# A decoder layer in one kernel: the page keys as three fp32r products of high and low parts

## The chip, the cores and the metric

The kernel runs on one core of one Trainium2 chip. The metric is the device time of a run in microseconds (us).

## What is computed

One layer of a hybrid decoder, for a prompt of 512 tokens and for 8 sequences with one new token each. Two parts of it meet in the stage that is changed. The first is the attention of the new tokens over 8 x 2048 cached positions, which lie in pages of 128 positions with a latent of 512 and a rotated key of 64 numbers:

```python
def mla_keys(ckv, kpe, w_uk, g_k):
    k_nope = jnp.einsum('...c,chd->...hd', ckv, w_uk)
    k_pe = jnp.broadcast_to(kpe[..., None, :], k_nope.shape[:-1] + (D_ROPE,))
    return rms_norm(jnp.concatenate([k_nope, k_pe], axis=-1), g_k)
...
        ckv_all = jnp.concatenate([cache_ckv[pages].reshape(past, D_LATENT), ckv_i], axis=0)
        k = mla_keys(ckv_all, kpe_all, w_uk, g_k)
        sc = jnp.einsum('qhd,khd->hqk', qi, k).astype(jnp.float32) * scale
        p = jax.nn.softmax(sc, axis=-1).astype(ckv_all.dtype)
        o_lat = jnp.einsum('hqk,kc->qhc', p, ckv_all)
```

The second is the mixer of experts for the prompt, 8 heads of 16 experts a token, so 128 slots for each of 4 tiles of 128 tokens:

```python
        act = jax.nn.gelu(jnp.einsum('thkd,td->thk', u_tab[ids], hb), approximate=False)
        return jnp.einsum('thk,thkd->td', g * act, v_tab[ids])
```

## The kernel before

The function `experts` holds the last stage. Each engine has its own program there, written out by hand as a loop over slots x (0 to 511 for the prompt, 16 more for the samples), and semaphores join them. In a slot GpSimd (POOL) gathers 128 rows of `peer_u` (into `u`, a ring of 4) and 128 rows of `peer_v` (into `v`, a ring of 8), 512 KB each. VectorE (DVE) forms the dot product with the token's row (line 2608), and 6 slots later adds the `v` row times its coefficient (line 2508). ScalarE (ACT) turns four dot products into coefficients with a gelu (line 2341), VectorE weights them (line 2621), and from slot 62 on every eighth `v` row is added by TensorE (PE, line 2140). VectorE also searches the experts of the units to come, 16 parts a unit, one part a slot.

The pages of the cache run in the same loop. Page g starts in slot `page_slot[g]` = 62 + 376 g / 128, so every 2.94 slots, 128 pages in slots 62 to 435, 16 pages a sequence. SyncE (SP) loads a page into a ring of 24 (lines 1986 to 1988), a reload waits until the sequence that held the place is weighed. In the slot of page g TensorE turns page g+1 (`turn`, 4 transposes at line 2109, one of the rotated keys at line 2110), and ScalarE copies the result into `ckvT` (line 2320) and `kpeT` (line 2321). `page_bank` forms the key products of page g in this slot and the next two, one PSUM bank a slot: 4 chunks of the latent times 392, 384 and 256 columns (384, 384 and 264 in every other sequence) of `wx`, which holds w_uk and on one side the queries folded through it; the product with the rotated queries stands at line 2127. ScalarE squares the heads of a bank one slot later (`page_squares`, line 2332, with its sum read in a second instruction) and copies the scores out (line 2334). At a sequence's end VectorE, ScalarE and TensorE make the softmax and the weighted sum (lines 2531 to 2555).

Engines follow their own order, so who waits holds up all that stands behind it. The gelu of a slot stands in ScalarE's program behind the squares of the slots before it, the squares wait for TensorE's bank (semaphore `keyed`), TensorE's bank waits until ScalarE has drained the same bank of the page before (`drained`), and VectorE waits for the coefficients (`gelued`).

A matmul of fp32 operands stands in the trace as two instructions. In the projections of the earlier stages the kernel already forms three fp32r products (`products`, lines 352 to 354) of operands that `lower` (line 346) has split into a rounded high part and the rest.

```python
    pe.matmul(out, w_hi, x_hi, start=first, stop=False)
    pe.matmul(out, w_hi, x_lo, start=False, stop=False)
    return pe.matmul(out, w_lo, x_hi, start=False, stop=last)
```

## Time and profile before

| | |
|---|---|
| runs | 2862.69, 2867.62, 2875.89 us |
| median | 2867.62 us |
| span of the profiled execution | 2876.5 us |
| own time of the profiled execution beside its span | not given apart; the span is used |
| mean granted TensorE clock | 0.917 |
| TensorE busy | 2433.7 us (85%) |
| VectorE busy | 2059.7 us (72%) |
| ScalarE busy | 916.1 us (32%) |
| GpSimd busy | 1410.3 us (49%) |
| stage `experts` | from about 1042 us to the end |
| pages | from about 1320 to 2580 us |

The span runs from the first to the last instruction of one profiled execution. Busy times are sums over all stages, which have different limits; a change in one stage has to be read in that stage. A matmul's end is modelled, so that TensorE's busy time is not its time at peak.

### The profile page before, as it was taken

What the parts mean: (1) busy time and instruction counts of PE and PEld (TensorE: products, weight loads), DVE (VectorE), ACT (ScalarE), POOL (GpSimd) and SP (SyncE); (2) the same over time, 40 slices, a digit from 0 to 9 for tenths busy, and PEclk for the clock granted to TensorE, in tenths of its full rate; (3) what the DMA queues carried; (4) which work ended last, traced back from release to release, by engine and by line L of the source; (5) the groups of instructions that cost most, each with busy time, mean ns of one, the idle gap of its engine ahead of it and who ended that gap; (6) DMA issues with size and microseconds to landing.
All of it is one profiled execution on the core that took longest, in us unless ns stands there. A gap on an engine that the chain in (4) does not pass through costs nothing.

```text
span 2876.5 us, 36363 instructions
## 1 busy us (share of the span) xinstructions
PE 2433.7 (85%) x11529; PEld 1646.0 (57%) x11529; DVE 2059.7 (72%) x4017; ACT 916.1 (32%) x3611; POOL 1410.3 (49%) x1184
## 2 busy tenths in 40 slices
PE   5999997968989986887999999989989989983353
PEld 3999997854456643444656556655655556552120
DVE  4665887955531118897887888887887879887687
ACT  3431003234330002213444444534444435440110
POOL 1121331210000005776767677767876667776575
PEclk8999998989999998998999999999999999995576
DMA  6324765544025558999989999898989899989997
GB/s 197 91 80 144 216 205 150 136 124 120 11 89 177 177 188 293 401 388 385 348 291 375 348 352 376 307 366 290 400 306 370 293 376 364 347 319 358 401 347 300
DMA packets 375326, 777.12 MB, mean 270 GB/s; under 512 B 46577, under 2 KB 181538, under 8 KB 375097
## 3 DMA queue, kind: packets, MB, share of 16 engines
q0 software_dynamic: 155568, 566.17, 52.7%
q1 hardware_dynamic: 198442, 183.99, 20.2%
q10 hardware_dynamic: 21124, 24.63, 2.6%
q8 instruction: 92, 1.51, 0.2%
q14 instruction: 100, 0.82, 0.1%
HBM read 745.38 MB, written 29.50 MB: 269 GB/s over the span
## 4 chain that ended last, share of the span: by engine, by line
PE 27%; issue 9%; another core or an unknown queue 9%; DMA 6%; DVE 4%; SPq 3%; POOL 2%; ACT 1%; POOLq 0%; DVEq 0%; ACTq 0%
PE mix_pair L2125 19%; DMA mix_u<-in_peer_u,mix_ids 5%; PE mix_pair L2048 2%; DVE mix_acc L2508 2%; PE mix_pair L2140 2%; POOL mix_v L2038 1%; DVE mix_u L2608 1%; SPq L1988 1%; PE mix_pair L2109 1%; DMA pag_kpe<-in_cache_kpe 1%; SPq L1987 1%; PE mix_pair L2127 1%; POOL mix_u L2031 1%; PE mix_pair L2077 1%
## 5 line engine op out<-in xcount | busy, mean ns | idle before, releaser
L2125 PE MATMUL mix_pair<-pag_wx,pag_ckvT 128*128 128x384 f32 (+3 forms) x3072 | 980.7, 467 | 39.4 <-issue 31.3
L2125 PEld LDWEIGHTS mix_pair<-pag_wx,pag_ckvT 128*128 128x128 f32 x3072 | 571.6, 194 | 336.1 <-issue 66.2
L2038 POOL DMA_INDIRECT mix_v<-in_peer_v,mix_ids x512 | 643.5, 1257 | 234.2 <-issue 171.0
L2031 POOL DMA_INDIRECT mix_u<-in_peer_u,mix_ids x512 | 595.6, 1163 | 316.7 <-issue 141.0
L2608 DVE CUSTOM_DVE_ANT_0 mix_u<-mix_u,mix_h 128x1024 f32<-128x1024 f32 x512 | 622.5, 1216 | 172.0 <-DMA mix_u<-in_peer_u,mix_ids 155.1
L2508 DVE SCALAR_TENSOR_TENSOR mix_acc<-mix_v,mix_coef,mix_acc 128x1024 f32<-128x1024 f32 x452 | 577.9, 1278 | 0.0
L2332 ACT ACTIVATE mix_pair<-mix_pair 128x128 f32<-128x128 f32 x1024 | 269.6, 263 | 445.3 <-PE mix_pair L2125 259.1
L379 POOL CAST inp_w_hi<-inp_w 128x1024 fp32r<-128x1024 f32 x74 | 112.2, 1517 | 377.1 <-DMA inp_w<-in_w_in 286.3
L2332 ACT ACTIVATION_READ_ACCUMULATOR mix_pair<-mix_pair 128x1 f32 x1024 | 191.7, 187 | 0.0
L2014 POOL IOTA mix_count_i<- 128x16 int32 x1 | 0.1, 134 | 376.2 <-POOLq L88 376.2
L2140 PE MATMUL mix_pair<-mix_v,mix_diag 128*128 128x512 f32 x224 | 116.5, 646 | 62.8 <-ACT mix_diag L2349 35.1
L352 PE MATMUL stp_ps<-inp_h_hi,inp_w_hi 128*128 128x260 f32 x512 | 148.0, 289 | 13.6 <-DVE inp_w_lo L346 10.4
L354 PE MATMUL stp_ps<-inp_h_hi,inp_w_lo 128*128 128x260 f32 x512 | 146.4, 286 | 0.0
L353 PE MATMUL stp_ps<-inp_h_lo,inp_w_hi 128*128 128x260 f32 x512 | 146.1, 285 | 0.0
L1677 DVE TENSOR_TENSOR mrg_gate<-mrg_psB,mrg_gate 128x520 f32<-128x520 f32 x8 | 5.6, 699 | 184.8 <-PE mrg_psB L1638 184.8
L2320 ACT ACTIVATE pag_ckvT<-mix_pair 128x512 f32<-128x512 f32 x128 | 75.6, 591 | 169.3 <-DMA scn_ce<-keep_acs 68.5
L2341 ACT ACTIVATE mix_coef<-mix_dots 128x4 f32<-128x4 f32 x128 | 25.9, 202 | 306.5 <-DVE mix_dots L2608 279.9
L352 PE MATMUL cnv_ps<-inp_h_hi,inp_w_hi 128*128 128x260 f32 x416 | 120.8, 290 | 0.0
L354 PE MATMUL cnv_ps<-inp_h_hi,inp_w_lo 128*128 128x260 f32 x416 | 118.4, 285 | 0.0
L353 PE MATMUL cnv_ps<-inp_h_lo,inp_w_hi 128*128 128x260 f32 x416 | 118.3, 284 | 0.0
L2077 PE MATMUL mix_pair<-chs_h2T,chs_wq 128*128 128x512 f32 (+2 forms) x352 | 115.9, 488 | 0.9 <-ACT chs_h2T L2304 0.6
L1638 PE MATMUL mrg_psB<-frt_x,mrg_wb 128*128 128x260 f32 x512 | 114.3, 384 | 0.0
(520 smaller groups left out, 4092.1 us busy)
## 6 DMA issues: line engine op xcount, KB each, us to landing
inp_w<-in_w_in SPq DMA_DIRECT2D x74, 512.0 KB, 4.2
pag_ckv<-in_cache_ckv SPq DMA_DIRECT2D x88, 256.0 KB
mrg_w_ada<-in_w_ada SPq DMA_DIRECT2D x8, 2048.0 KB, 9.9
chs_wq<-in_peer_wq SPq DMA_DIRECT2D x11, 1024.0 KB, 16.5
all_shared<-in_cache_ckv SPq DMA_DIRECT2D x40, 256.0 KB
keep_proj<-stp_out ACTq DMA_DIRECT2D x32, 260.0 KB
ada_w_ada<-in_w_ada SPq DMA_DIRECT2D x4, 2048.0 KB, 12.8
stp_st<-in_state_ssm POOLq DMA_DIRECT2D x8, 1024.0 KB, 6.9
```

The source lines that it names most:

```text
L352: pe.matmul(out, w_hi, x_hi, start=first, stop=False)
L353: pe.matmul(out, w_hi, x_lo, start=False, stop=False)
L354: return pe.matmul(out, w_lo, x_hi, start=False, stop=last)
L1638: last = pe.matmul(psB[:, b, s, 0:HALF], wb[:, b, k, :], yT[:, k, s * HALF:(s + 1) * HALF], start=(k == 0), stop=(k == KI - 1))
L2031: pool.indirect_dma_start(u[:, x % UR, :], None, u_rows, bass.IndirectOffsetOnAxis(at, 0)).then_inc(u_in[x % UR], 16)
L2038: pool.indirect_dma_start(v[:, y % VR, :], None, v_rows, bass.IndirectOffsetOnAxis(at, 0)).then_inc(v_in[y % VR], 16)
L2077: last = pe.matmul(bank[2 + side][:, 0:w], wq[:, n % 2, k, side * P:(side + 1) * P], h2T[:, k, cols], start=(k == 0), stop=(k == KD - 1))
L2125: last = pe.matmul(to, ckvT[:, g % 2, k, :], wx[:, k, lo:hi], start=(k == 0), stop=(k == KL - 1))
L2140: last = pe.matmul(psV[:, c, :], diag[:, d % 2, :], v[:, r, c * 512:(c + 1) * 512], start=(x == first_on_pe[t]), stop=(x == last_on_pe[t]))
L2332: last = act.activation(psN[j][:, at:at + NOPE], psN[j][:, at:at + NOPE], ACT.Square, accum_out=ss[:, b % 2, t, h:h + 1])
L2508: dve.scalar_tensor_tensor(acc[:, :], v[:, r, :], c, acc[:, :], ALU.mult, ALU.add).then_inc(v_used[r], 1)
L2608: dve.tensor_tensor_reduce(u[:, r, :], u[:, r, :], h2[:, t % 2, :], 1.0, 0.0, ALU.mult, ALU.add, dots[:, t % 2, slot:slot + 1]).then_inc(u ...
```

## The change

The key products of a page are made of three fp32r products in place of one fp32 product. Both operands are split: `wx` into `wx_hi` (ScalarE rounds) and `wx_lo` (VectorE subtracts, line 346), in slots 24 to 41 for w_uk, and a slot after each copy of a sequence's queries. A page's high part `ckvT_hi` is the copy that ScalarE makes of the turned page, rounded on writing. One slot after the turn, TensorE multiplies it by minus the identity (`minus`) on top of the turned page in the same PSUM bank, which leaves the rest there, and ScalarE copies that as `ckvT_lo`. The next page's turn waits for that copy.

The second set of operands takes room. Four places of the ring of pages move into the scores of tile 0 (`sc_first`), and SP loads them only when that tile's 8 units are searched; `w_uk` is loaded into `shared`, and the first page waits until it is split; `ids` and `gate` keep two tiles, not four; `hot` shares the place of the two candidate tiles; w_uv is loaded behind all pages; the samples' small tiles lie where the pages were, so their zeroing and loads come after the last page, and `mul_s` is made at TAIL + 8, not TAIL + 2 (TAIL is slot 460). The scores of tile 0 and 1 are copied apart.

```diff
-            SHARED = 8
-            ckv, kpe = e.sb("ckv", [P, NPG - SHARED, LAT]), e.sb("kpe", [P, NPG, ROPE])
+            SHARED, SCORED = 8, 4
+            ckv, kpe = e.sb("ckv", [P, NPG - SHARED - SCORED, LAT]), e.sb("kpe", [P, NPG, ROPE])
             ckv_shared = shared[:, :].rearrange("p (r c) -> p r c", r=SHARED)
-            ckvT, kpeT = e.sb("ckvT", [P, 2, KL, P]), e.sb("kpeT", [ROPE, 2, P])
-            wx = e.sb("wx", [P, KL, WX])
+            ckv_scored = flat2(sc_first[:, :]).rearrange("p (r c) -> p r c", r=SCORED)
+            ckvT_hi, ckvT_lo = e.sb("ckvT_hi", [P, 2, KL, P], F32R), e.sb("ckvT_lo", [P, 2, KL, P], F32R)
+            kpeT, minus = e.sb("kpeT", [ROPE, 2, P]), e.sb("minus", [P, P], F32R)
+            e.sb("unused", [P, P])
+            wx_lo, wx_hi = e.sb("wx_lo", [P, KL, WX], F32R), e.sb("wx_hi", [P, KL, WX], F32R)
+            w_uk = shared[:, :].rearrange("p (k n) -> p k n", k=KL)
...
-        score_of = lambda unit: sc[:, unit]
-        page_rows = lambda r: ckv[:, r, :] if r < NPG - SHARED else ckv_shared[:, r - (NPG - SHARED), :]
+        score_of = lambda unit: sc_first[:, unit] if unit < PH else sc[:, unit - PH]
+        OWN = NPG - SHARED - SCORED
+        page_rows = lambda r: ckv[:, r, :] if r < OWN else ckv_shared[:, r - OWN, :] if r < OWN + SHARED else ckv_scored[:, r - OWN - SHARED, :]
...
-        score_rows = sc[:, :, :, :].rearrange("p (t h) s n -> p t h s n", t=TT)
+        score_rows = sc[:, :, :, :].rearrange("p (t h) s n -> p t h s n", t=TT - 1)
+        scores_to = lambda ts, h: sc_first[:, h:h + 1] if ts[0] == 0 else score_rows[:, ts[0] - 1:ts[0] - 1 + len(ts), h]
...
+        rest_at = {page_slot[0] - 1: 0, **{x + 1: g + 1 for g, x in enumerate(page_slot) if g + 1 < PAGES}}
+        queries_at = {page_slot[NT * (b - 1) + 1]: b for b in range(2, TS)}
+        WX_AT = (24, 29, 35, 40)
...
             sp.wait_ge(res_summed, 2 * TT)
-            sp.dma_start(wx[:, :, QW:QW + H * NOPE], heads("w_uk")).then_inc(wx_in, 16)
+            sp.dma_start(w_uk, heads("w_uk")).then_inc(wx_in, 16)
...
             sp.wait_ge(scored, len(steps))
+            sp.wait_ge(wx_lowered, KL)
             for g in range(PAGES):
+                if g == OWN + SHARED:
+                    sp.wait_ge(found, PARTS * PH)
                 if g >= NPG:
                     sp.wait_ge(weighed, (g - NPG) // NT + 1)
-                if g == PAGES - 24:
-                    sp.wait_ge(found, PARTS * 16)
-                    sp.dma_start(w_uv, heads("w_uv")).then_inc(uv_in, 16)
                 page = sp.value_load(table[0:1, g:g + 1], min_val=0, max_val=A["cache_ckv"].shape[1] - 1)
                 sp.dma_start(page_rows(g % NPG), A["cache_ckv"][0, bass.ds(page, 1)].rearrange("a p c -> (a p) c")).then_inc(page_in[g % NPG // 4], 16)
                 sp.dma_start(kpe[:, g % NPG, :], A["cache_kpe"][0, bass.ds(page, 1)].rearrange("a p c -> (a p) c")).then_inc(page_in[g % NPG // 4], 16)
             sp.wait_ge(found, PARTS * 24)
-            sp.dma_start(gate1_s, ada_s(2)).then_inc(gate1_in, 16)
-            sp.dma_start(mul_s, ada_s(4)).then_inc(scale_in, 16)
+            sp.dma_start(w_uv, heads("w_uv")).then_inc(uv_in, 16)
             sp.wait_ge(y_stored, 16 * (TT - 1))
             sp.dma_start(gain_s, A["g_ffn"].to_broadcast([TS, D])).then_inc(scale_in, 16)
             sp.wait_ge(weighed, TS)
+            sp.dma_start(mul_s, ada_s(4)).then_inc(scale_in, 16)
             sp.dma_start(w_a[:, :, :], wide("w_br_a")).then_inc(a_in, 16)
+            sp.dma_start(gate1_s, ada_s(2)).then_inc(gate1_in, 16)
+            sp.dma_start(x1s[:, :], A["x_sample"].rearrange("b t d -> (b t) d")).then_inc(x1s_in, 16)
             sp.dma_start(w_out_lo[:, :, :], wide("w_out")[:, 0:KD // 2, :]).then_inc(out_in, 16)
             sp.dma_start(w_out_hi, wide("w_out")[:, KD // 2:KD, :]).then_inc(out_in, 16)
             sp.wait_ge(muls_made, 1)
...
             def turn(g):
                 r = g % NPG
                 pe.wait_ge(page_in[r // 4], 128 * (g // NPG + 1))
-                after(pe, copied, 2 * g)
+                after(pe, copied, 3 * g)
                 for k in range(KL):
-                    pe.transpose(psT[:, k * P:(k + 1) * P], page_rows(r)[:, k * P:(k + 1) * P], K["ident"][:, :])
+                    pe.matmul(psT[:, k * P:(k + 1) * P], page_rows(r)[:, k * P:(k + 1) * P], K["ident"][:, :], start=(k == 0), stop=(k == KL - 1), is_transpose=True,
+                              skip_group_check=True)
                 pe.transpose(psK[0:ROPE, 0:P], kpe[:, r, :], K["ident"][:, :]).then_inc(turned, 1)
+
+            def page_rest(g):
+                pe.wait_ge(copied, 3 * g + 2)
+                pe.wait_ge(negated, 1)
+                pe.matmul(psT, minus[:, :], ckvT_hi[:, g % 2].rearrange("p k n -> p (k n)"), start=False, stop=True, skip_group_check=True).then_inc(rest_made, 1)
             def page_bank(g, j):
                 b, odd = g // NT, g // NT % 2
                 lo, hi = ((QW * odd, 392), (392, 776), (776, WX - QW * (1 - odd)))[j]
                 if j == 0:
                     if g % NT == 0:
-                        pe.wait_ge(q_set, b + 1)
+                        pe.wait_ge(q_low, b + 1)
                     if g == 0:
-                        pe.wait_ge(wx_in, 16)
+                        pe.wait_ge(wx_lowered, KL)
                         pe.wait_ge(s_copied, scores_before[-1])
-                    pe.wait_ge(copied, 2 * g + 2)
+                    pe.wait_ge(copied, 3 * g + 3)
                 after(pe, drained, 3 * (g - 1) + j + 1)
                 to = psN[j][:, QW * odd * (j == 0):QW * odd * (j == 0) + hi - lo]
                 for k in range(KL):
-                    last = pe.matmul(to, ckvT[:, g % 2, k, :], wx[:, k, lo:hi], start=(k == 0), stop=(k == KL - 1))
+                    last = products(pe, to, (ckvT_hi[:, g % 2, k, :], ckvT_lo[:, g % 2, k, :]), (wx_hi[:, k, lo:hi], wx_lo[:, k, lo:hi]), k == 0, k == KL - 1)
                     if k == 0 and j == 2 * odd:
                         pe.matmul(psN[0][:, 0:QW] if not odd else psN[2][:, 256:256 + QW], kpeT[:, g % 2, :], L["q_rope"][:, b, :],
                                   start=False, stop=False)
                     g = page_at[x]
                     if g + 1 < PAGES:
                         turn(g + 1)
+                if x in rest_at:
+                    page_rest(rest_at[x])
                 for g, j in bank_at.get(x, ()):
                     page_bank(g, j)
...
             def page_copy(g):
                 act.wait_ge(turned, g + 1)
                 after(act, keyed, 3 * (g - 1))
-                act.activation(ckvT[:, g % 2].rearrange("p k n -> p (k n)"), psT, ACT.Copy).then_inc(copied, 1)
+                act.activation(ckvT_hi[:, g % 2].rearrange("p k n -> p (k n)"), psT, ACT.Copy).then_inc(copied, 1)
                 act.activation(kpeT[:, g % 2, :], psK[0:ROPE, 0:P], ACT.Copy).then_inc(copied, 1)
+
+            def page_rest(g):
+                act.wait_ge(rest_made, g + 1)
+                act.activation(ckvT_lo[:, g % 2].rearrange("p k n -> p (k n)"), psT, ACT.Copy).then_inc(copied, 1)
...
+                if x in WX_AT:
+                    k = WX_AT.index(x)
+                    act.wait_ge(wx_in, 16)
+                    act.activation(wx_hi[:, k, QW:QW + H * NOPE], w_uk[:, k, :], ACT.Copy).then_inc(wx_rounded, 1)
...
                     page_squares(g, j)
+                if x in rest_at:
+                    page_rest(rest_at[x])
                 if x == page_slot[0] - 2:
+                    act.activation(minus[:, :], K["ident"][:, :], ACT.Copy, scale=-1.0).then_inc(negated, 1)
                     page_copy(0)
...
                         residual(t)
                     if x == NORM_AT[t]:
                         norm(t)
+                if x - 1 in WX_AT:
+                    k = WX_AT.index(x - 1)
+                    lower(dve, wx_hi[:, k, QW:QW + H * NOPE], wx_lo[:, k, QW:QW + H * NOPE], w_uk[:, k, :], wx_rounded, wx_lowered, k + 1)
+                if x == 31:
+                    for b in range(2):
+                        cols = slice(0, QW) if b == 0 else slice(WX - QW, WX)
+                        lower(dve, wx_hi[:, :, cols], wx_lo[:, :, cols], L["q_lat"][:, :, b, :], q_set, q_low, b + 1)
+                if x - 1 in queries_at:
+                    b = queries_at[x - 1]
+                    cols = slice(0, QW) if b % 2 == 0 else slice(WX - QW, WX)
+                    lower(dve, wx_hi[:, :, cols], wx_lo[:, :, cols], L["q_lat"][:, :, b, :], q_set, q_low, b + 1)
...
-                if x == TAIL + 2:
+                if x == TAIL:
+                    dve.tensor_copy(mineT[:, :, :], K["ident"][0:TS, 0:TS].unsqueeze(1).to_broadcast([TS, P // TS, TS]))
+                if x == TAIL + 8:
                     dve.wait_ge(scale_in, 32)
                     dve.scalar_tensor_tensor(mul_s, mul_s, 1.0, gain_s, ALU.add, ALU.mult).then_inc(muls_made, 1)
```

TensorE's program, two slots of a page in the first sequence (`all_ident` the identity, `pag_wx` the weights, `pag_ckvT` the turned page; the last number is the columns). Before:

```order
L2109 MATMUL mix_pair<-all_ident,pag_ckv 128x128 x4
L2110 MATMUL mix_pair<-all_ident,pag_kpe 64x128
L2125 MATMUL mix_pair<-pag_wx,pag_ckvT 128x392
L2127 MATMUL mix_pair<-all_q_rope,pag_kpeT 128x8
L2125 MATMUL mix_pair<-pag_wx,pag_ckvT 128x392 x3
L2125 MATMUL mix_pair<-pag_wx,pag_ckvT 128x384 x4
```

After, from the rope product of a page to the first product of its second bank:

```order
L2146 MATMUL mix_pair<-all_q_rope,pag_kpeT 128x8
L352 MATMUL mix_pair<-pag_wx_hi,pag_ckvT_hi 128x392
L353 MATMUL mix_pair<-pag_wx_lo,pag_ckvT_hi 128x392
L354 MATMUL mix_pair<-pag_wx_hi,pag_ckvT_lo 128x392
...
L2129 MATMUL mix_pair<-pag_ckvT_hi,pag_minus 128x512
L352 MATMUL mix_pair<-pag_wx_hi,pag_ckvT_hi 128x384
```

Each product has become three, and the product that makes the rest of the page turned last (line 2129) stands between the first bank and the second.

ScalarE's program around one page (`mix_coef<-mix_dots` is the gelu, `mix_ss` the squares' sums). Before:

```order
L2320 ACTIVATE pag_ckvT<-mix_pair 128x512
L2321 ACTIVATE pag_kpeT<-mix_pair 64x128
L2388 ACT_TABLE_LOAD
L2388 ACTIVATE mix_exps,mix_total<-mix_exps 128x16
L2341 ACT_TABLE_LOAD
L2341 ACTIVATE mix_coef<-mix_dots 128x4
L2328 ACTIVATE mix_kpe_sq,mix_kss<-pag_kpe 128x64
L2332 ACTIVATE mix_pair,mix_ss<-mix_pair 128x128 x8
```

After:

```order
L2341 ACTIVATE pag_ckvT_hi<-mix_pair 128x512
L2342 ACTIVATE pag_kpeT<-mix_pair 64x128
L2374 ACTIVATE mix_diag<-all_ident,mix_coef 128x128
L2353 ACTIVATE mix_pair,mix_kss<-pag_kpe 128x64
L2357 ACTIVATE mix_pair,mix_ss<-mix_pair 128x128 x3
L2346 ACTIVATE pag_ckvT_lo<-mix_pair 128x512
L2366 ACTIVATE mix_coef<-mix_dots 128x4
L2357 ACTIVATE mix_pair,mix_ss<-mix_pair 128x128 x3
```

The copy of the rest (line 2346) stands behind the squares of the first bank, and here ahead of a gelu.

## Rows read from the trace of the kernel before

**Rows 1.** The page of the profile, its first line.
```profile
span 2876.5 us, 36363 instructions
```

**Rows 2.** Windows: busy us (x instructions) by engine, clock, DMA.
```profile
core 0: us, PE busy (x) PEld busy (x) DVE busy (x) ACT busy (x) POOL busy (x), PEclk, DMA share, GB/s
1200.00:1320.00 120.00, 85.95 (x284) 48.99 (x283) 105.67 (x203) 21.28 (x48) 92.59 (x76) 0.87 1.02 387
1320.00:2580.00 1260.00, 1183.19 (x4470) 737.57 (x4470) 1038.19 (x2088) 571.41 (x2967) 902.72 (x743) 0.97 0.92 345
```

**Rows 3.** Windows of line 2608 alone, two records a slot.
```profile
1200.00:1320.00 120.00, 45.40 (x74) 0.87 1.02 387
1320.00:2580.00 1260.00, 455.98 (x746) 0.97 0.92 345
```

**Rows 4.** Waits of VectorE, 1320 to 2580 us: us, times, longest.
```profile
DVE mix_u L2608 <- DMA mix_u<-in_peer_u,mix_ids: 85.8, 89, 3.2
DVE mix_coef L2621 <- ACT mix_coef L2341: 56.2, 14, 8.0
DVE mix_rstd L2534 <- ACT mix_rstd L2379: 34.0, 5, 9.1
DVE mix_u L2608 <- issue: 13.2, 22, 2.1
DVE all_o_lat L2555 <- remote: 11.2, 3, 4.4
DVE mix_coef L2621 <- issue: 10.3, 4, 6.7
DVE mix_rstd L2531 <- ACT mix_raw L2334: 4.3, 2, 3.4
DVE mix_rstd L2531 <- issue: 3.7, 1, 3.7
DVE mix_part_sum L2548 <- ACT mix_s L2382: 3.1, 3, 1.6
```

**Rows 5.** Timeline around 2084 to 2104 us: start, us, instruction, idle before.
```profile
2083.53 4.47 PE L2125 MATMUL mix_pair<-pag_wx,pag_ckvT 128*128 128x384 f32 x16
2089.54 2.24 PE L2125 MATMUL mix_pair<-pag_wx,pag_ckvT 128*128 128x392 f32 x6
2087.26 0.26 ACT L2332 ACTIVATE mix_pair<-mix_pair 128x128 f32<-128x128 f32 x1 [2.65 <-PE mix_pair L2125]
2092.26 0.26 ACT L2332 ACTIVATE mix_pair<-mix_pair 128x128 f32<-128x128 f32 x1 [4.01 <-PE mix_pair L2125]
2099.41 0.26 ACT L2332 ACTIVATE mix_pair<-mix_pair 128x128 f32<-128x128 f32 x1 [5.92 <-remote]
2103.13 0.16 DVE L2621 TENSOR_TENSOR mix_coef<-mix_coef,mix_gate 128x4 f32<-128x4 f32 x1 [5.47 <-ACT mix_coef L2341]
```

**Rows 6.** Timeline of TensorE, one page from turn to turn.
```profile
1904.20 0.60 PE L2109 MATMUL mix_pair<-all_ident,pag_ckv 128*128 128x128 f32 x4
1904.75 5.77 PE L2125 MATMUL mix_pair<-pag_wx,pag_ckvT 128*128 128x384 f32 x18
1910.45 0.38 PE L2127 MATMUL mix_pair<-all_q_rope,pag_kpeT 64*128 64x8 f32 x2
1910.77 1.60 PE L2125 MATMUL mix_pair<-pag_wx,pag_ckvT 128*128 128x264 f32 x6
1912.20 0.60 PE L2109 MATMUL mix_pair<-all_ident,pag_ckv 128*128 128x128 f32 x4
```

**Rows 7.** Timeline of TensorE in the projection, three fp32r products a chunk.
```profile
401.45 0.28 PE L353 MATMUL stp_ps<-inp_h_lo,inp_w_hi 128*128 128x260 f32 x1
...
403.95 0.28 PE L353 MATMUL stp_ps<-inp_h_lo,inp_w_hi 128*128 128x260 f32 x1
```

**Rows 8.** Groups by line and form, whole span: busy us, mean ns.
```profile
L2125 PEld LDWEIGHTS mix_pair<-pag_wx,pag_ckvT 128*128 128x128 f32 x3072 | 571.6, 194 | 336.1 <-issue 66.2 <-ACT mix_pair L2332 11.0 <-ACT mix_raw L2334 6.0
L346 DVE TENSOR_TENSOR inp_w_lo<-inp_w,inp_w_hi 128x1024 fp32r<-128x1024 f32 x74 | 96.8, 1319 | 16.1 <-POOL inp_w_hi L379 15.7
L2320 ACT ACTIVATE pag_ckvT<-mix_pair 128x512 f32<-128x512 f32 x128 | 75.6, 591 | 169.3 <-DMA scn_ce<-keep_acs 68.5 <-PE mix_pair L2110 63.3 <-PE mix_pair L2125 20.5
```

70 lines of the change are left out of this document (36 added, 34 removed).

## The prediction

> **What bounds the kernel now.** I first looked for the stretch in which the page products stand. The windows [rows 2] show it from 1320 to 2580 us: 1260 us, with TensorE busy 1183 us (94%), VectorE 1038 us (82%), the DMA queues at 0.92 of their time and 345 GB/s. Nothing is at its limit on its own. In the 120 us ahead of it, with no pages, TensorE is at 72%, VectorE at 88% and the queues at 1.02 and 387 GB/s. The instructions of the dot product alone [rows 3] give the pace: two records are one slot, so 37 slots in 120 us (3.24 us each) and 373 slots in 1260 us (3.38 us each). The first number is the higher for its bytes: weights for the queries are loaded there.
>
> VectorE carries each slot, so its idle time is what can be won. Its waits in the stretch [rows 4] fall in two parts. It waits for gathered rows 85.8 + 13.2 = 99 us. It waits for something that ScalarE has to deliver 56.2 + 34.0 + 11.2 + 10.3 + 4.3 + 3.7 + 3.1 = 122.8 us, in 14 + 5 + 3 + 4 + 2 + 1 + 3 = 32 waits, 3.8 us each. 1038 + 99 + 123 is the stretch of 1260 us (one more wait, of 2.5 us, is not among the rows). ScalarE itself is busy less than half of it (571 us in [rows 2]). It is late because the squares of a page stand ahead of the gelu in its order, and they wait for TensorE.
>
> [Rows 5] show one such case, and with it the doubtful point of this forecast. TensorE's 16 instructions from 2083.53 (the second and third bank of a page) have ended by 2088.00, and those of 2089.54 belong to the next page's first bank. ScalarE begins the squares of the first bank at 2087.26, of the second at 2092.26 and of the third (two heads, the last of the page) at 2099.41, waiting 2.65, 4.01 and 5.92 us, though by its records TensorE was done 4 us and 11 us before the last two. VectorE then stands 5.47 us for the coefficients. So a part of the 123 us is not TensorE working too long, but its word arriving late at ScalarE, and shorter products do not shorten that.
>
> **The change, part by part.** *Key products.* [Rows 6] hold one page from turn to turn: 1904.20 to 1912.20, 8.00 us. The transposes take 0.55 (to 1904.75), the rope product 0.32 (1910.45 to 1910.77), and 7.13 us are left for the 12 fp32 products over 4 x (384 + 384 + 264) = 4128 columns, 1.73 ns a column. Three fp32r products of the same kind as the new ones (high x high, low or high weights changing at each) run in the projection [rows 7]: from the record at 401.45 to that at 403.95, 21 products of 260 columns in 2.50 us, 0.119 us each, 0.458 ns a column. Three are 1.37 ns a column, 5.67 us a page. That frees 1.46 us. If the part of a product that does not grow with its columns is large, 384 columns cost less than this line says; 5.4 us is the other end.
>
> A rule of the Trainium skill speaks against the change: TensorE: Matmul & The Clock Gate, "Measured speedup vs the span model", says that a weight load overlaps a running product only when the row groups differ. By it, and the same page's 128 / 1.2 = 107 ns a load (my estimate from the page's figures), the page's 36 loads would lie bare: 3.9 us, and a page would take longer than before. The trace disagrees: the 0.119 us of [rows 7] hold product and load.
>
> *The low part.* One product of 512 columns at 0.458 ns is 0.23 us. Net: 1.46 - 0.23 = 1.2 us a page, 128 pages: 156 us less work for TensorE, 1027 us in place of 1183. It would be busy about 85% of a stretch of 1210 us. At 72% the granted clock was 0.87, here it is 0.97 [rows 2]: even 0.93 would give back only 4% of 1027 us, which the slack covers.
>
> *ScalarE.* One more copy of 128x512 a page, 591 ns [rows 8]: 128 x 0.59 = 76 us more, 647 us of 1260. It stands behind the first bank's squares, ahead of the next gelu. On its own it is covered.
>
> *One more handover.* Before, TensorE turned page g+1, and needed ScalarE's copy three slots later. Now, one slot later, it must make the rest from that copy before it may start the second bank of page g, and ScalarE must wait for the rest before it goes on to the gelu. The handovers from TensorE to ScalarE go from 4 to 5 a page, and this one has a slot of cover, not three. Queued behind it on TensorE are two banks, behind ScalarE's wait the squares and the gelu, for which VectorE waits. Its price does not stand in the trace: the near bound is nothing (0.6 us of copy behind 1.9 us of products), the far one 4.01 us [rows 5]. I take it in the sum as eating part of the relief, below.
>
> *VectorE.* Four low parts of w_uk, 128x1024, 1319 ns each [rows 8]: 5.3 us, at slots 25 to 41, where it is idle 12% of the time; I charge 3 us. ScalarE's four rounding copies are hidden there. Eight small low parts of the queries: some 1 us in all. Five more score copies and the moved memsets, which were 3 small ones ahead of the stage: nothing, under VectorE's 12% idle and the gathers.
>
> *Queues.* SP loads 20 pages at first, not 24; pages 20 to 23 wait for the 8th search (slot 103), and are turned from slot 117 on. 14 slots x 3.38 = 47 us are in hand for 4 pages. If that cover went, the price would be a burst of 4 pages, 1.15 MB, at 345 GB/s: 3.3 us. w_uv comes behind the last page, at about slot 420 for slot 460. In the tail mul_s comes after the last weighing, and VectorE forms it at TAIL+8, two slots before anything needs it late. The bytes of the tail are the same. I put all this at nothing.
>
> **The sum.** How much of the 123 us comes back? Not less than nothing, not more than all of it. The case in [rows 5] says that the waits consist of TensorE's lateness plus late arrival. A page now is 1.2 us shorter, and between the slot at which TensorE falls behind and VectorE's wait lie one or two pages: 1.2 x 1.4 = 1.7 us less in each of 32 waits, 54 us. Less 4 us for VectorE's added work: 50 us. The profiled execution has a span of 2876.5 us [rows 1]; it would come to 2826.5. The runs shown have a median of 2867.62, 8.9 us under that span, so I forecast **2818 us**. A difference under 0.5% (14 us) can't be told from no change.
>
> **Rivals.**
> - *Everything comes back.* If TensorE's load is the whole cause, VectorE will be idle only as much as ahead of the pages: 105.67 of 120 us busy, and 1038 / 0.881 = 1179 us, a gain of 81 less 4, so 2790. With every one of the 123 us gone it is 2749. For it: TensorE at 94%. Against it: ScalarE's waits that begin after TensorE's records end. I give 0.22 to 2743 to 2793.
> - *Nothing measurable.* The late words decide alone, or the gathers take back what ScalarE gives: the 434 MB of the stretch (1260 us x 345 GB/s) at 387 GB/s need 1123 us, so the queues do not forbid a gain, and this is less likely. 2853 to 2882, chance 0.15.
> - *Slower: the added handover.* A page waits twice in series for TensorE's word (turned, then rest), and TensorE sends more instructions (36 products in place of 24 records a page). If one page in four takes an extra 4.01 us on VectorE's path, 32 x 4 = 128 us stand against 50, so 2868 + 78 = 2946. It decides from 64 us on, one page in eight. For it: 2.65, 4.01 and 5.92 us in one page. Against: the first bank's 1.9 us lie between copy and rest. Chance 0.25.
> - *Bare weight loads.* Twelve more loads a page at 194 ns each [rows 8] would cost 2.3 us, 1.1 more than the page wins, 140 us in all if TensorE then sets the pace: 3008. The rule named above is this one; [rows 7] leave it 0.02.
> - The forecast itself, 2793 to 2853, has 0.36.
>
> **The numbers.** Faster by over 0.5%: 0.36 + 0.22 = 0.58. Within: 0.15. Slower: 0.27. The range 2765 to 2895 leaves out about 0.07 below, where nearly all of the 123 us would have to come back, and about 0.12 above, where the handover fails at more than one page in seven.
>
> **What would show it.** In the profile after: the records of a page's products from turn to turn 6.8 us apart where TensorE is not held up (wrong if above 7.3); TensorE's share of the stretch near 85%; VectorE's waits for ScalarE near 70 us, in place of 123, and its waits for gathered rows at 99 or more. If TensorE now waits for the copy at the new product (an idle row of over 50 us there), or ScalarE for the rest, the slower rival is at work. If the stretch ends 80 us or more sooner, the lateness of TensorE's word was only its load. The forecast is wrong too if the clock falls below 0.9 in the stretch, or if the pages 20 to 23 are late.

## The result

The changed kernel takes 2905.54 us (median of 4 runs, 2897.26 to 2928.30), the kernel before 2869.88 on the same chip (4 runs, 2862.69 to 2875.89). The ratio is 1.0126 [1.0084, 1.0168]: 36 us slower, where 50 us faster was forecast. The forecast missed, on the sign too.

The page of the changed kernel, its first line, one of its three groups of key products, and the new product of 512 columns (L2129):

```profile
span 2896.7 us, 39969 instructions
...
L352 PE MATMUL mix_pair<-pag_wx_hi,pag_ckvT_hi 128*128 128x384 f32 (+3 forms) x1536 | 545.1, 355 | 5.6 <-issue 2.8
...
L2129 PE MATMUL mix_pair<-pag_ckvT_hi,pag_minus 128*128 128x512 f32 x128 | 64.9, 507 | 113.6 <-ACT pag_kpeT L2342 87.6
```

The profiled execution is 20.2 us longer than that before (2896.7 against [rows 1]); the other 16 us of the difference of medians are seen in no trace. TensorE's idle time stands at L2129, where it waits for ScalarE's copy of the page that it has turned.

The windows of the same two stretches as [rows 2]:

```profile
core 0: us, PE busy (x) PEld busy (x) DVE busy (x) ACT busy (x) POOL busy (x), PEclk, DMA share, GB/s
1200.00:1320.00 120.00, 91.55 (x308) 51.09 (x306) 115.09 (x222) 26.04 (x60) 92.45 (x78) 0.92 1.03 391
1320.00:2580.00 1260.00, 1089.21 (x6076) 956.43 (x6077) 1030.57 (x2084) 625.91 (x3055) 905.19 (x741) 0.92 0.93 344
```

In the stage TensorE fell from 94% to 1089 / 1260 = 86%, as forecast. VectorE did no more in the same 1260 us than before (1031 us, 1038 before). So 94 us less of TensorE's time bought VectorE nothing. Its waits tell what happened to the 122.8 us of [rows 4]:

```profile
engine line waited for: us in total, times, longest us
DVE mix_u L2653 <- DMA mix_u<-in_peer_u,mix_ids: 72.0, 73, 2.7
DVE mix_coef L2666 <- ACT mix_coef L2366: 58.2, 12, 8.1
DVE mix_u L2653 <- issue: 34.3, 47, 2.6
DVE pag_wx_lo L346 <- ACT pag_wx_hi L2408: 25.5, 4, 9.1
DVE pag_wx_lo L346 <- issue: 7.4, 2, 5.6
DVE mix_part_sum L2591 <- ACT mix_s L2414: 7.1, 3, 3.2
DVE mix_rstd L2574 <- ACT mix_pair L2357: 6.6, 2, 4.2
DVE all_o_lat L2598 <- remote: 5.5, 2, 2.8
```

What the forecast counted as ScalarE's is waited for 58.2 + 25.5 + 7.4 + 7.1 + 6.6 + 5.5 us in these rows. With the small ones that are left out (3.6 + 3.1 + 2.1 + 1.6 + 1.0) it is 122 us, as much as before. The old waits did shrink, to 89 us, and 33 us stand at a new place: L346, the low parts of the queries, where VectorE waits for ScalarE's high part. I had put that edit at some 1 us in all. Rows are waited for 106 us, 99 before. One of the groups, `all_o_lat`, isn't ScalarE's: VectorE waits there for a product of TensorE (semaphore `o_turned`), 11.2 us before and 5.5 + 3.6 = 9.1 us now.

TensorE's timeline of a page, one product to a row (start, duration, instruction, idle time before it):

```profile
start us, us, engine line op out<-in xcount [idle before <-releaser]
...
1603.00 0.60 PE L2122 MATMUL mix_pair<-all_ident,pag_ckv 128*128 128x128 f32 x4
...
1604.07 0.34 PE L352 MATMUL mix_pair<-pag_wx_hi,pag_ckvT_hi 128*128 128x384 f32 x1
...
1605.13 0.34 PE L352 MATMUL mix_pair<-pag_wx_hi,pag_ckvT_hi 128*128 128x384 f32 x1
...
1605.49 0.33 PE L354 MATMUL mix_pair<-pag_wx_hi,pag_ckvT_lo 128*128 128x384 f32 x1
1606.33 0.50 PE L2129 MATMUL mix_pair<-pag_ckvT_hi,pag_minus 128*128 128x512 f32 x1 [0.51 <-issue]
...
1610.75 0.49 PE L2122 MATMUL mix_pair<-all_ident,pag_ckv 128*128 128x128 f32 x3
```

From turn to turn (L2122) 7.75 us pass. Of these about 0.7 go to the wait ahead of L2129 (the next product could have begun at 1605.66), so the page alone takes some 7.1, under the 7.3 at which the step would have been wrong. Six products with their own weight loads stand between 1604.07 and 1605.13: 0.177 us each, 0.46 ns a column at a granted clock of 1.00, as taken from [rows 7]. By the rule of the Trainium skill that I weighed (TensorE: Matmul & The Clock Gate; it stands in "The mechanism", not in the section that the prediction names) the loads would lie bare; the trace disagrees here too. The same section of the Trainium skill also lets a load into the background weight buffer run ahead, a case that I left out; the trace shows the overlap, and not which buffer was loaded.

The same place in the program as [rows 5], first TensorE, then ScalarE, then VectorE:

```profile
2084.54 0.34 PE L354 MATMUL mix_pair<-pag_wx_hi,pag_ckvT_lo 128*128 128x392 f32 x1
2084.72 0.40 PE L2129 MATMUL mix_pair<-pag_ckvT_hi,pag_minus 128*128 128x512 f32 x1
...
2086.89 0.34 PE L354 MATMUL mix_pair<-pag_wx_hi,pag_ckvT_lo 128*128 128x384 f32 x1
...
2088.37 0.28 PE L354 MATMUL mix_pair<-pag_wx_hi,pag_ckvT_lo 128*128 128x256 f32 x1
2093.76 1.09 PE L2122 MATMUL mix_pair<-all_ident,pag_ckv 128*128 128x128 f32 x4 [5.11 <-ACT pag_ckvT_lo L2346]
```
```profile
2092.13 0.26 ACT L2357 ACTIVATE mix_pair<-mix_pair 128x128 f32<-128x128 f32 x1 [8.31 <-remote]
...
2093.02 0.59 ACT L2346 ACTIVATE pag_ckvT_lo<-mix_pair 128x512 fp32r<-128x512 f32 x1
2099.28 0.26 ACT L2357 ACTIVATE mix_pair<-mix_pair 128x128 f32<-128x128 f32 x1 [5.67 <-remote]
```
```profile
2103.37 0.16 DVE L2666 TENSOR_TENSOR mix_coef<-mix_coef,mix_gate 128x4 f32<-128x4 f32 x1 [7.13 <-ACT mix_coef L2366]
```

The first bank's last product ends at 2084.88. ScalarE, idle, begins that bank's squares at 2092.13, 7.25 us later. The second bank's products were over by 2087.23, and its squares begin at 2099.28, 5.67 us after ScalarE's last instruction. TensorE stands 5.11 us for the low copy (L2346), and VectorE 7.13 us for the coefficients (5.47 in [rows 5]). Nothing that TensorE computes is late here by these records; its word is. The trace also keeps the time of each semaphore's update: the one for the first bank stands at 2092.11, 7.23 us after the bank's last record and 0.02 us before the squares.

I counted these late words in the traces: a square of a bank, or the copy of a turned page, that begins over 0.6 us after both the last product's record and ScalarE's own last instruction have ended. The usual distance is 0.04 us. For a copy, the products of the page two before it must have ended too, for it waits for their word as well. The changed kernel has 72 late ones among 384 first squares of a bank (189 us) and 19 among 128 copies (49 us). The kernel before has 54 (136 us) and 25 (72 us). For 71 of the 72, an update of the bank's semaphore is recorded within 0.04 us before the squares begin: TensorE's word comes late, ScalarE doesn't start late.

VectorE gets late words from TensorE too. In the kernel before all 11.2 us of `all_o_lat` in [rows 4] are three such waits, in the changed one 5.5 us are two, the first of them (`remote` is explained at the last set of runs):

```profile
1868.28 0.19 DVE L2598 TENSOR_TENSOR all_o_lat<-mix_pair,mix_share 128x32 f32<-128x32 f32 x1 [2.68 <-remote]
```

### The profile page after: what moved, and what is told of

The parts are those of the page before. It is cut to its first block, busy times and chain, and to the rows that moved or that the text cites. A ratio compares the mean times of both kernels' runs of the same rounds, so it can differ in the third digit from the quotient of the medians.

```text
span 2896.7 us, 39969 instructions
## 1 busy us (share of the span) xinstructions
PE 2348.5 (81%) x13193; PEld 1875.7 (65%) x13193; DVE 2063.5 (71%) x4029; ACT 983.9 (34%) x3749; POOL 1413.3 (49%) x1184
## 4 chain that ended last, share of the span: by engine, by line
PE 17%; issue 13%; DVE 12%; DMA 10%; POOL 4%; another core or an unknown queue 3%; ACT 3%; SPq 1%; POOLq 0%; ACTq 0%; DVEq 0%
DMA mix_u<-in_peer_u,mix_ids 7%; DVE mix_acc L2540 5%; DVE mix_u L2653 5%; PE mix_pair L354 3%; PE mix_pair L352 3%; PE mix_pair L353 3%; POOL mix_u L2044 2%; POOL mix_v L2051 2%; PE mix_pair L2061 2%; DMA all_shared<-in_peer_keys 1%; ACT mix_pair L2357 1%; PE mix_pair L2159 1%; PE mix_pair L2090 1%; PE mix_pair L2122 1%
## 5 line engine op out<-in xcount | busy, mean ns | idle before, releaser
L2044 POOL DMA_INDIRECT mix_u<-in_peer_u,mix_ids x512 | 608.0, 1188 | 312.4 <-issue 145.1
L2051 POOL DMA_INDIRECT mix_v<-in_peer_v,mix_ids x512 | 632.1, 1235 | 250.9 <-issue 173.9
L352 PE MATMUL mix_pair<-pag_wx_hi,pag_ckvT_hi 128*128 128x384 f32 (+3 forms) x1536 | 545.1, 355 | 5.6 <-issue 2.8
L353 PE MATMUL mix_pair<-pag_wx_lo,pag_ckvT_hi 128*128 128x384 f32 (+3 forms) x1536 | 512.6, 334 | 3.4 <-issue 3.4
L354 PE MATMUL mix_pair<-pag_wx_hi,pag_ckvT_lo 128*128 128x384 f32 (+3 forms) x1536 | 512.4, 334 | 1.0 <-issue 1.0
L352 PEld LDWEIGHTS mix_pair<-pag_wx_hi,pag_ckvT_hi 128*128 128x128 f32 x1536 | 307.1, 200 | 13.7 <-issue 6.5
L353 PEld LDWEIGHTS mix_pair<-pag_wx_lo,pag_ckvT_hi 128*128 128x128 f32 x1536 | 307.2, 200 | 13.5 <-issue 7.1
L354 PEld LDWEIGHTS mix_pair<-pag_wx_hi,pag_ckvT_lo 128*128 128x128 f32 x1536 | 306.0, 199 | 5.1 <-issue 5.0
L2129 PE MATMUL mix_pair<-pag_ckvT_hi,pag_minus 128*128 128x512 f32 x128 | 64.9, 507 | 113.6 <-ACT pag_kpeT L2342 87.6
```

What stands on the lines that cost most here:

```text
L2044: pool.indirect_dma_start(u[:, x % UR, :], None, u_rows, bass.IndirectOffsetOnAxis(at, 0)).then_inc(u_in[x % UR], 16)
L2051: pool.indirect_dma_start(v[:, y % VR, :], None, v_rows, bass.IndirectOffsetOnAxis(at, 0)).then_inc(v_in[y % VR], 16)
L2129: pe.matmul(psT, minus[:, :], ckvT_hi[:, g % 2].rearrange("p k n -> p (k n)"), start=False, stop=True, skip_group_check=True).then_inc(res ...
```

## The experiments

There are five sets of runs behind the first pair, each set on a chip of its own, and the chips are of two kinds. On three (first, third and fourth set) the kernel before takes 2805 to 2807 us, and no traced kernel has a late square (defined above); the kernel before itself has no trace there. In the first pair and on the other two (second and fifth set) it takes 2870 to 2905 us, and every trace has 47 or more. Each ratio is against the kernel before on the same chip.

**The parts of the change.** Two kernels leave out part of the computation: the first keeps of the three products high x high alone, the second leaves out the product that makes the low part, so that ScalarE's low copy takes the whole value. The third forms one fp32 product of the high parts (their low parts are left out), and keeps every handover.

```diff
-  last = products(pe, to, (ckvT_hi[:, g % 2, k, :], ckvT_lo[:, g % 2, k, :]), (wx_hi[:, k, lo:hi], wx_lo[:, k, lo:hi]), k == 0, k == KL - 1)
+  last = pe.matmul(to, ckvT_hi[:, g % 2, k, :], wx_hi[:, k, lo:hi], start=(k == 0), stop=(k == KL - 1))
...
-  if x in rest_at:
-      page_rest(rest_at[x])
-  act.wait_ge(rest_made, g + 1)
...
+  last = pe.matmul(to, ckvT_hi[:, g % 2, k, :].bitcast(F32), wx_hi[:, k, lo:hi].bitcast(F32), start=(k == 0), stop=(k == KL - 1))
```

> The changed kernel, but of the three products of a chunk only high x high is formed (the low parts are still made, copied and handed over; the keys lose the low terms). TensorE loses 24 of 36 products a page, some 3.8 us of 8 us. Theory 'load' (TensorE's own work sets the pace of the page stage, and the forecast's relief was merely too small or spent elsewhere): 2780 to 2830 us, and VectorE's waits for ScalarE fall below 60 us. Theory 'late word' (ScalarE is held by TensorE's signals arriving late, whatever TensorE has to do): 2880 to 2910 us. Theory 'handover' (the wait of TensorE for the copy ahead of the second bank, and of ScalarE for the rest, sets the pace): also 2880 to 2910 us, with TensorE's idle time at the rest product growing well beyond 110 us.

> The changed kernel without the product by minus the identity: ScalarE makes its second copy from the turned page itself, at the same place in its order and with no wait for TensorE, and TensorE does not wait for the first copy before the second bank (the low part then holds the whole value). Products, copies and bytes are as in the changed kernel. Theory 'handover': the 110 us of TensorE's idle time ahead of that product go, and the time falls to 2810 to 2850 us. Theory 'late word': signals stay late at the squares, 2885 to 2910 us. Theory 'load': one product of 0.23 us less a page, 2890 to 2905 us.

> The changed kernel, but the three fp32r products of a chunk are one fp32 product of the high parts, as heavy as the product before the change (the low terms are left out of the keys). The rest product, both copies and the handover stay. So it has the load of the kernel before and the handover of the changed one. Theory 'load': TensorE gets 1.4 us a page more than in the changed kernel, 2980 to 3060 us. Theory 'late word', if lateness grows with the number of TensorE's instructions (24 records of products a page, not 36): 2870 to 2895 us; if it does not depend on them: 2905 us. Theory 'handover': 2905 to 2935 us, a little over the changed kernel since the first bank covers it no better.

Measured: before 2806.71; high x high alone 2793.06, ratio 0.9954 [0.9938, 0.9970]; no handover 2794.95, 0.9967 [0.9948, 0.9985]; fp32 2834.30, 1.0114 [1.0087, 1.0142]. This chip is of the first kind, and the times expected were priced from the other kind, so they decide little here. With two thirds of the changed kernel's products taken away the time is half a per cent under the kernel before; what bounds it is not TensorE.

**The change again, with two orders moved.** One run repeats the change. One has VectorE form the queries' low parts 11 slots later, to be rid of the wait at L346; one makes the rest of a page a slot later as well, ahead of the turn. One more run of the kernel before is beside them, for its trace.

```diff
-                if x - 1 in queries_at:
+                if x - 12 in queries_at:
...
-        rest_at = {page_slot[0] - 1: 0, **{x + 1: g + 1 for g, x in enumerate(page_slot) if g + 1 < PAGES}}
+        rest_at = {page_slot[0] - 1: 0, **{x + 2: g + 1 for g, x in enumerate(page_slot) if g + 1 < PAGES}}
```

> The changed kernel once more, beside the kernel before on one chip and with the next two. The first comparison gave 2905.54 against 2869.88 us; on the chip of the last three experiments the kernel before took 2806.71 us and no signal of TensorE reached ScalarE late. Theory 'late word': the ratio depends on whether signals arrive late. Where they do not, the changed kernel stands at 0.995 to 1.003 (2793 to 2815 if the kernel before takes 2807), where they do, at 1.01 again. Theory 'fixed cost' (the added waits of VectorE and ScalarE cost the same everywhere): 1.01 on any chip.

> The changed kernel, but VectorE makes the low part of a sequence's queries 12 slots after ScalarE's rounding of them, not one slot (they are used 15 pages, so some 44 slots, later). In the profile after VectorE waits there 25.5 + 7.4 us for ScalarE. Theory 'VectorE's new wait': where that wait stands in the profile, all of it comes back, 25 to 33 us less than the changed kernel; on a chip without late signals, where the experiments showed 0.5 and 4.0 us there (25.8 us with the heavier products), 0 to 8 us less. Rival: VectorE would have waited at the next coefficient or row anyway, 0 to 5 us less on any chip.

> The last kernel, and besides the rest product and its copy stand one slot later, ahead of the third bank in place of the second, so that TensorE has two banks of cover for ScalarE's first copy. Theory 'handover': TensorE's idle time at the rest product (113 us in the profile after) falls to below 40 us, and the time falls by 10 to 30 us against the last kernel where signals are late, by up to 10 us where not. Rival 'TensorE's idle time costs nothing' (the gathers and VectorE set the pace): within 5 us of the last kernel; or slower, up to 15 us, since the rest now stands right ahead of the next turn and holds it.

> The kernel before, for its trace on this chip. Theory 'late word': where its time is near 2807 us, no squares begin over 0.6 us after both their bank's end and ScalarE's own last instruction (54 cases, 136 us, in the first trace), VectorE's waits for ScalarE fall from 123 to below 50 us, the DMA queues stand at 0.97 or more of the page stage, and TensorE is busy over 95% of it. Theory 'load': the waits for ScalarE stay near 123 us.

Measured, on a chip of the second kind (before 2905.36): the change 2944.61, 1.0191 [1.0135, 1.0246]; queries later 2953.96, 1.0200 [1.0141, 1.0259]; rest later too 2971.62, 1.0267 [1.0204, 1.0331]; the one run of the kernel before 2893.23. Waits of VectorE with the queries later, 1320 to 2540 us:

```profile
DVE mix_coef L2666 <- ACT mix_coef L2366: 110.7, 21, 8.8
...
DVE mix_rstd L2577 <- ACT mix_rstd L2411: 41.3, 5, 12.0
```

The wait at L346 is gone (it was 22.7 us in the repeat), but the coefficients rose from 91.7 to 110.7 us and the roots at L2577 from 0.2 to 41.3. These two traces are of a long run and a short one (2985.25 and 2928.14 us, medians 2953.96 and 2944.61), so a part of that rise is the run's. The medians are enough: 25 to 33 us were expected back, and none came. So that wait was where the lateness surfaced, not its cause: my guess of a fixed cost there fell. With the rest later, TensorE's wait at the rest product fell to 13.8 us, as expected, but it waits 106.6 us at its turn for the low copy, 36 times (1320 to 2540 us), and by the median the kernel is slower still (the intervals touch): the place in the change was the better one, or no worse.

**The parts on a chip without late words.** Beside them a version of the kernel before whose gathers leave out every second row of v from slot VR on, so that its output lacks them; the waits for `v` are counted to match.

```diff
+                    if left_out(y):
+                        continue
```

> The changed kernel beside the kernel before, for whichever kind of chip this is. Signals late (the kernel before at 2870 to 2905 us): 1.010 to 1.022. No signal late (near 2807): theory 'late word' expects 0.995 to 1.003, since without its second product handover it stood at 0.9967 there; theory 'fixed cost' expects 1.01 again.

> High x high alone, as in the first experiment, now beside the changed kernel on the same chip. Where signals are late: theory 'lateness grows with the number of TensorE's instructions while the queues are full' (12 products a page in place of 36) expects the late squares to fall from some 75 cases and 200 us to below 30 cases and 70 us, and a time under the kernel before, 0.97 to 0.985. Theory 'lateness comes from the full queues alone' expects 70 cases or more and 1.00 to 1.02. Where no signal is late: 0.995 again.

> Without the rest product and its handover, as in the second experiment (the low part holds the whole value). Where signals are late: theory 'handover' expects it at or under the kernel before, 0.99 to 1.00, 1.5 to 2 per cent under the changed kernel. Theory 'number of instructions' expects it within 0.6 per cent of the changed kernel, since 37 products a page become 36. Where no signal is late: 0.997 again.

> The kernel before with every second gather of a row of the second table left out from slot 8 on (the add runs on an old row): three quarters of the gathers' bytes, all of the engines' work. Theory 'late word from full queues': no or hardly any late signals even on a chip that has them (below 10 cases in place of 54 to 63), and the page stage as short as TensorE and VectorE allow, 8.95 us a page, 1146 to 1180 us in place of 1257; the time falls by 120 to 200 us. Rival 'TensorE's density alone makes them late': 50 cases or more.

Measured (before 2805.11): the change 2797.23, 0.9966 [0.9948, 0.9983]; high x high alone 2796.62, 0.9968 [0.9952, 0.9984]; no handover 2798.90, 0.9967 [0.9952, 0.9982]; fewer rows 2726.07, 0.9714 [0.9680, 0.9747]. Here the change is a third of a per cent faster, and no part of it costs anything that shows. The theory of a fixed cost, 1.01 on any chip, fell. The windows of the change and of its waits:

```profile
1320.00:2540.00 1220.00, 1073.55 (x6158) 945.53 (x6158) 1082.33 (x2188) 641.45 (x3114) 951.00 (x775) 0.94 0.99 370
```
```profile
DVE mix_u L2653 <- DMA mix_u<-in_peer_u,mix_ids: 122.8, 137, 4.1
DVE mix_coef L2666 <- ACT mix_coef L2366: 5.4, 2, 4.2
DVE mix_part_sum L2591 <- ACT mix_s L2414: 4.2, 3, 2.3
DVE mix_rstd L2577 <- ACT mix_rstd L2411: 1.9, 2, 1.7
DVE pag_wx_lo L346 <- ACT pag_wx_hi L2408: 1.1, 3, 0.6
```

The queues are at 0.99, VectorE at 1082 / 1220 = 89%, and what it still waits for is gathered rows: 122.8 of 135.4 us. With fewer rows (1320 to 2500 us) another engine ends the waits:

```profile
1320.00:2500.00 1180.00, 1137.74 (x4418) 715.00 (x4420) 1052.70 (x2149) 567.82 (x2919) 702.92 (x573) 0.98 0.83 287
```
```profile
DVE mix_coef L2633 <- ACT mix_coef L2353: 61.6, 17, 8.3
DVE mix_rstd L2546 <- ACT mix_rstd L2391: 33.1, 7, 6.8
DVE mix_u L2620 <- DMA mix_u<-in_peer_u,mix_ids: 18.2, 21, 4.1
```

TensorE is at 1138 / 1180 = 96%. So on such a chip the kernel before has two bounds 3% apart, first the queues, then TensorE, and less work for TensorE alone never brought it below 0.995. The fall of 79 us is less than the 120 to 200 us expected. What fewer rows do to late words was not tested: this chip has none.

**The fourth set, with the fp32 form again.** Same edits.

> The changed kernel beside the kernel before and the next three. Where no signal is late: 0.9966 again (0.994 to 0.999). Where they are late: 1.010 to 1.022.

> High x high alone. Where signals are late: theory 'lateness grows with TensorE's instructions' expects late squares below 30 cases and 70 us, and a ratio of 0.97 to 0.985; theory 'full queues alone' 60 cases or more and 1.00 to 1.02. Where none is late: 0.995 to 0.998.

> Without the rest product and its handover. Where signals are late: theory 'handover' 0.99 to 1.003; theory 'number of instructions' within 0.6% of the changed kernel. Where none is late: 0.995 to 0.998.

> One fp32 product of the high parts, with the rest product and its handover: the product load and records of the kernel before (24 a page), the handover of the changed one. Where signals are late: theory 'number of instructions' expects late squares back at the 54 to 63 cases of the kernel before, and, its load being 0.23 us a page over it, 1.01 to 1.02; theory 'handover' 1.02 to 1.04. Where none is late: 1.011 again.

Measured, none late again (before 2805.61): 2800.46, 0.9966 [0.9945, 0.9986]; 2794.72, 0.9959 [0.9941, 0.9978]; 2800.14, 0.9982 [0.9962, 1.0002]; fp32 2837.82, 1.0096 [1.0063, 1.0128]. The window of the fp32 form:

```profile
1320.00:2540.00 1220.00, 1195.59 (x4613) 755.44 (x4613) 1043.94 (x2104) 638.73 (x3104) 925.43 (x751) 0.99 0.97 359
```

TensorE at 1196 / 1220 = 98% is the bound. With the rest product and both copies kept, the three fp32r products alone are worth 2837.82 - 2800.46 = 37 us here. The low part costs 2837.82 - 2805.61 = 32 us as long as the products are in fp32. The two nearly cancel. That the queues cut off what remains is argued from their 0.99 and from high x high alone, which is only 6 us faster than the change (2794.72).

**The parts on a chip with late words.** Same edits.

> The changed kernel. Where signals are late 1.010 to 1.022, where not 0.994 to 0.999.

> High x high alone. Where signals are late: theory 'lateness grows with TensorE's instructions' expects below 30 late squares and 0.97 to 0.985; theory 'full queues alone' 60 or more and 1.00 to 1.02. Where none is late: 0.995 to 0.998.

> Without the rest product and its handover. Where signals are late: theory 'handover' 0.99 to 1.003; theory 'number of instructions' within 0.6% of the changed kernel. Where none is late: 0.995 to 0.999.

Measured (before 2870.01): the change 2918.63, 1.0161 [1.0069, 1.0253]; high x high alone 2833.25, 0.9860 [0.9788, 0.9933]; no handover 2882.71, 1.0065 [1.0025, 1.0105]. Windows of the change and of high x high alone, and ScalarE's waits in each for TensorE's words:

```profile
1320.00:2540.00 1220.00, 1049.92 (x5804) 917.47 (x5804) 985.79 (x1997) 598.69 (x2916) 851.79 (x709) 0.92 0.93 339
```
```profile
ACT mix_pair L2357 <- PE mix_pair L354: 214.4, 146, 5.0
ACT mix_pair L2357 <- remote: 174.8, 50, 11.7
ACT pag_ckvT_hi L2341 <- remote: 55.6, 18, 11.2
```
```profile
1320.00:2540.00 1220.00, 755.88 (x3077) 566.79 (x3075) 1044.14 (x2107) 630.86 (x3104) 918.62 (x751) 0.74 0.96 359
```
```profile
ACT pag_ckvT_hi L2341 <- remote: 102.9, 21, 19.4
ACT mix_pair L2357 <- PE mix_pair L2144: 70.5, 56, 4.2
...
ACT mix_pair L2357 <- remote: 47.5, 26, 7.8
```

"remote" stands where the view finds nothing on this core that ended the wait; late words fall under it. On the chips without them there is no such row. For the squares it is 174.8 us here and 47.5 with a third of the products; for the copies of the turned page it is 55.6 and 102.9, so that the two together fall from 230 to 150 us.

Neither theory on the number of instructions or on the queues alone has its range met by high x high alone: 47 late squares and 100 us stand between "below 30 and 70 us" and "60 or more", 0.9860 just above 0.985. Nor do the two theories on the kernel without the handover: 1.0065 is above 1.003, and 1% under the changed kernel, not within 0.6%.

The count of late words of each traced kernel (late of 384 squares, their us; late of 128 copies, their us; both over the whole stage), with TensorE in the stage:

| kernel, chip kind | TensorE busy us, matmuls (in) | squares | copies | ratio |
|---|---|---|---|---|
| before, first pair | 1183, 4470 (1260) | 54, 136 | 25, 72 | 1 |
| changed, first pair | 1089, 6076 (1260) | 72, 189 | 19, 49 | 1.0126 |
| before, second set | 1185, 4468 (1260) | 63, 173 | 28, 67 | 1 |
| changed, second set | 1066, 5944 (1260) | 79, 209 | 27, 79 | 1.0191 |
| queries later | 1040, 5678 (1260) | 85, 270 | 36, 89 | 1.0200 |
| rest later too | 1053, 5778 (1260) | 82, 255 | 26, 56 | 1.0267 |
| changed, fifth set | 1050, 5804 (1220) | 83, 235 | 24, 50 | 1.0161 |
| no handover, fifth set | 1059, 5818 (1220) | 73, 240 | 26, 63 | 1.0065 |
| high x high, fifth set | 756, 3077 (1220) | 47, 100 | 24, 75 | 0.9860 |
| all kernels, chips without | | 0, 0 | 0, 0 | |

The places aren't random. Of the 72 late squares of the changed kernel in the first pair, 34 are late at the same bank in the second set and 37 in the fifth, where independent places would give some 15. So what runs at a place matters, and not the chip alone.

## Why the prediction was wrong

- *What bounds the kernel.* Half right. The doubtful point of [rows 5] was the main matter: the squares come late because a word is late. And behind ScalarE stood a second bound that I had put aside with "the queues do not forbid a gain". The two stretches of [rows 2] showed it at 1.02 in the slots without pages.
- *Key products and low part.* Right: 0.46 ns a column, 7.1 us a page. TensorE gave back 94 us in the same 1260, and 86% of the stage is left where 85% was forecast.
- *ScalarE.* 626 us against 571, 55 more in equal windows, not 76; it is idle half of the time, and harmless in itself: on the chips without late words it cost nothing that shows.
- *The added handover.* On the chips without late words the kernel that leaves it out is no faster (0.9967 and 0.9982 against 0.9966 twice). On the one chip with them it is 36 us faster than the change (2918.63 - 2882.71), though the intervals of the two ratios overlap (1.0069 to 1.0105). Its sign, over 50 us of idle time at the new product, came true (113.6 us), though 47 us of waiting stand there on a chip without late words too (third set), at no cost. So the slower rival is partly borne out, and only on the chips with late words: it takes the product and its wait away together, and which of them counts isn't told apart. Even without them the kernel stays at 1.0065, over 1.
- *VectorE.* The waits of `all_o_lat` were taken for ScalarE's and are TensorE's, 11.2 of the 122.8 us. The eight query low parts, "some 1 us in all", were mis-sized: 33 us of waiting in the first pair. On the chips without late words it is 1.1 and 1.9. Moving the wait away returned nothing.
- *Queues and the tail.* Nothing of the moved page loads shows. By the starts of the dot products the changed trace is 6.6 us behind at slot 0, 8.2 us at slot 62, where the pages begin, 0.3 us at slot 117, where the late-loaded pages start to be turned, 15.5 us at slot 448, after their end, and 19.5 us at the last slot: the page stage holds some 7 of the 20 us. The rest lies outside it in this pair of traces, and isn't explained.
- *The sum.* This is the step that failed: "1.7 us less in each of 32 waits, 54 us". It took VectorE's waits to shorten with TensorE's load. Their sum went from 122.8 to 122 us, with 94 us less work on TensorE. The waits for late words didn't shrink with the load; they grew, from 54 to 72 squares (and from 63 to 79 in the second set), while TensorE's busy time fell. So its load alone doesn't set them. What grew is the number of its instructions, 4470 to 6076, and with it the handovers of a page; the kernel with 3077 has the fewest late squares. These counts are from one trace a kernel and chip, and how far they move from run to run isn't known; the six kernels with nearly the full number of products give 72 to 85 among themselves. That the number is the cause is argued from this order alone: no experiment changed the number with all else kept, and the fp32 form ran only on chips without late words.
- *The rivals.* "Nothing measurable" named both limits rightly, late words and gathers, and is what the chips without late words show (0.9966 is within 0.5%). It took the late words as given, though, not as something that the change makes more of.

Why TensorE's words come late, and on some chips alone, is open. What the traces exclude: in the first pair ScalarE's start after VectorE's dots is never over 0.04 us late in the same stage, so ScalarE isn't slow to start; and TensorE starts within 0.15 us of ScalarE's word in the changed kernel. Late are the words that TensorE sends, to ScalarE and to VectorE. The episode above lies where the queues run at 1.02 and 398 GB/s (2082 to 2090 us). In the whole stage they are at 0.93, and at 0.99 on the chips without late words, so full queues alone don't do it either.

One more difference between the chips stands in the traces. Each of the changed kernel's five traces records all 39969 instructions, but 23229 to 23843 updates of semaphores on the chips with late words and 33468 to 33475 on the others; of the 384 words for banks 327 to 335 have an update of their own recorded, against all 384. The records are alike up to about 1200 us and thin out in the stage of the gathers. Whether updates merge there or their records are lost isn't told, and no run excludes that the recording itself has a part in the lateness.

## What to carry to other kernels

Before pricing a faster engine, look whether the waits that cost begin after that engine's records have ended: if so, its busy time isn't what is waited for, and shorter work may buy nothing, while more instructions and handovers may cost (argued here, not shown). Read the next limit from the stretch without the work that is sped up, and cut the gain there: here it was the queues, half a per cent away. Where a trace shows such late words, compare on more than one chip, since the sign of this change depends on it (0.9966 or 1.0126 to 1.0191).

## What the runs showed of the hardware

- The same kernel before took 2805 to 2807 us in three sets and 2870 to 2905 us in two sets and the first pair. In the latter words from TensorE come late, up to 7.5 us for a bank in the first pair and 11.7 us in the fifth set, and to VectorE too (2.7 and 2.8 us in the changed kernel); in the other three sets no square is late, and with the changed kernel the queues move 368 to 370 GB/s in the stage in place of 336 to 344.
- At a granted clock of 1.00 an fp32r product with its weight load takes 0.46 ns a column at 260 and at 384 columns, and an fp32 product 1.73 ns: three products of parts cost four fifths of the one in fp32.
- With high x high alone, in the first set, TensorE was busy 748 of 1220 us (61%) at a granted clock of 0.76 in the stage, and the kernel still had the lowest median of its set (2793.06 us).
- In the stage of the gathers the changed kernel's traces on the chips with late words hold 327 to 335 updates for its 384 words for banks, those on the others all 384, with the same instructions recorded.
